# Second sample batch's logits in the last prompt step's slot, and two scale buffers in the second attention

## The reference

```python
fox_o = fox_prompt(fq, fk, fv, flf)                    # 8 heads x 64, causal, logits + forget bias
dsa_o = dsa_prompt(dq, iq, iw, dk, dv, ik, topk_prompt)  # 8 query heads on 2 kv heads, 256 picked keys
mix = jnp.concatenate([fox_o, dsa_o], axis=-1) @ w_out[l]
yp = post_sublayers(yp, mix, ...)                      # LN, FFN, LN
fox_s = fox_sample(gq, gk, gv, glf, cache_fox_k[l], cache_fox_v[l], cache_fox_logf[l])
dsa_s = dsa_select_attend(eq, jq, jw, pos_s, k_all, v_all, ik_all, kpos_s, topk_sample)
mix_s = jnp.concatenate([fox_s, dsa_s], axis=-1) @ w_out[l]
ys = post_sublayers(ys, mix_s, ...)
```

## Time and profile before

| what | us |
|---|---|
| three runs of before | 1408.16, 1414.36, 2643.92 (median 1414.36) |
| profiled execution, its own time | 1406.06 |
| its span, first to last instruction | 1404.2 |
| PE, PEld, DVE, ACT, POOL busy | 1343.7 (96%), 1199.1 (85%), 971.0 (69%), 686.7 (49%), 545.3 (39%) |
| mean granted PE clock | 0.991 of full speed |

### The profile page before, as it was taken

How to read it: one execution, slowest core, us unless ns; L and a number is a source line. 1 busy time by engine, 2 the same in 40 slices (tenths; PEclk the granted TensorE clock), 3 DMA queues, 4 the chain that set the end, 5 groups by cost and what they waited for, 6 DMA issues and landing times.

```text
span 1404.2 us, 23682 instructions
## 1 busy us (share of the span) xinstructions
PE 1343.7 (96%) x8916; PEld 1199.1 (85%) x8916; DVE 971.0 (69%) x1801; ACT 686.7 (49%) x1250; POOL 545.3 (39%) x518
## 2 busy tenths in 40 slices
PE   7989999989996999999989999999999999999997
PEld 7869999977775777787789999999999997678886
DVE  4489998878883889657866455555645557856498
ACT  5569989648773888611252232333223334524331
POOL 2407675512232022423465555555555551010011
PEclk9999999999998999999999999999999999999999
DMA  7202433349836312510134354355335459747454
GB/s 239 58 17 77 144 104 112 75 114 229 207 100 169 96 41 54 188 48 31 46 129 152 127 163 144 130 173 173 131 125 166 147 190 378 250 155 240 165 178 152
DMA packets 150354, 197.19 MB, mean 140 GB/s; under 512 B 28104, under 2 KB 106856, under 8 KB 150240
## 3 DMA queue, kind: packets, MB, share of 16 engines
q1 hardware_dynamic: 150240, 195.67, 44.6%
HBM read 136.69 MB, written 48.38 MB: 132 GB/s over the span
## 4 chain that ended last, share of the span: by engine, by line
PE 52%; DVE 3%; DMA 2%; issue 1%; ACT 1%; POOL 0%; POOLq 0%; SPq 0%; DVEq 0%; ACTq 0%
PE ffn L2760 31%; PE ffn L2269 6%; PE ffn L2860 4%; PE ffn L2862 4%; PE ffn L2861 4%; DMA down_raw<-in_w_down 1%; DVE rows L3256 1%; PE ffn L2734 1%; DVE down_lo L3125 0%; DMA up_raw<-in_w_up 0%; ACT down_hi L3016 0%; PE ffn L2879 0%; PE ffn L2877 0%; DVE h_T_lo L3160 0%; PE ffn L2285 0%
## 5 line engine op out<-in xcount | busy, mean ns | idle before, releaser
L3041 POOL TENSOR_TENSOR w_lo<-w_S,w_hi 128x512 fp32r<-128x512 f32 x88 | 119.2, 1355 | 108.9 <-ACT w_hi L2916 108.9
L2760 PE MATMUL ffn<-h_T_hi,w_hi 128*128 128x264 f32 x704 | 144.7, 285 | 0.2 <-DVE h_T_lo L3160 0.2
L3016 ACT CAST down_hi<-down_raw 128x1024 fp32r<-128x1024 f32 (+1 forms) x77 | 89.9, 1173 | 110.7 <-DMA down_raw<-down_w 46.2
L2760 PE MATMUL ffn<-h_T_lo,w_hi 128*128 128x264 f32 x704 | 143.7, 285 | 0.0
L2760 PE MATMUL ffn<-h_T_hi,w_lo 128*128 128x264 f32 x704 | 142.9, 283 | 0.0
L2916 ACT CAST w_hi<-w_S 128x512 fp32r<-128x512 f32 x88 | 54.8, 622 | 167.0 <-PE ffn L2760 147.4
L2173 POOL TENSOR_TENSOR ln_rstd<-ln_var_eps,ln_power 128x1 f32<-128x1 f32 (+1 forms) x18 | 29.4, 1633 | 272.9 <-DVE ln_var_eps L2153 141.0
L3125 DVE TENSOR_TENSOR down_lo<-down_raw,down_hi 128x1024 fp32r<-128x1024 f32 (+1 forms) x77 | 106.2, 1401 | 29.0 <-ACT down_hi L3016 28.3
L2860 PE MATMUL ffn<-down_hi 128*128 128x512 f32 x308 | 120.8, 392 | 3.7 <-DVE down_lo L3125 2.0
L2862 PE MATMUL ffn<-down_hi,down_lo 128*128 128x512 f32 x308 | 120.5, 391 | 0.0
L2861 PE MATMUL ffn<-down_lo,down_hi 128*128 128x512 f32 x308 | 120.4, 391 | 0.0
(11 more groups left out here) (423 smaller groups left out, 3841.5 us busy)
## 6 DMA issues: line engine op xcount, KB each, us to landing
down_raw<-down_a SPq DMA_DIRECT2D x77, 256.0 KB, 3.5
gate_raw<-in_w_gate SPq DMA_DIRECT2D x11, 1024.0 KB, 6.5
up_raw<-in_w_up SPq DMA_DIRECT2D x11, 1024.0 KB, 6.3
down_t<-in_w_down SPq DMA_DIRECT2D x44, 256.0 KB, 4.1
down_w<-down_t SPq DMA_DIRECT2D x22, 512.0 KB, 3.4
down_raw<-in_w_down SPq DMA_DIRECT2D x22, 512.0 KB, 6.2
down_raw<-down_w SPq DMA_DIRECT2D x44, 256.0 KB, 4.0
down_a<-down_s SPq DMA_DIRECT2D x10, 1024.0 KB, 4.1
```

What stands on the lines that cost most here:

```text
L2760: mm = nc.tensor.matmul(pp[:, bank[to] + ch, 0:PIECE], l, x[name][:, k, ch * PIECE:(ch + 1) * PIECE], start=opens and k == 0 and i == 0, s ...
L3016: nc.scalar.copy(hs[:, 0:n], raws[s % RAWS][:, 0:n]).then_inc(hi_done, 1)
L3041: nc.gpsimd.tensor_tensor(w_lo[n % 2][:, :, :], weight(m, SCHEME[q][0]), f32(w_hi[n % 2][:, :, :]), ALU.subtract).then_inc(w_lo_done, 1)
```

## The change

Three edits. First, in both attentions the logits of sample batch 17 move from slot L+3 to slot L, behind the last prompt step's transposes. Second, `attention` takes a list of scale buffers; the first attention gives it one, the second two, so that there SP waits for the multiplication two batches back. Third, to make room for the second buffer, `dsa_kT_new` and `dsa_q_diag` lie in another region of SBUF. The numbers of idle products stay as they are.

```diff
 def fox_ahead(batches):
     def ahead(batch):
         if batch.sample:
-            return [(1, 0, len(batch.parts) - 1)]
+            return [(1, 0, -1)]
...
-    [(1, 0, 2)]]
+    [(1, 0, -1)]]
...
+    scales_loaded = [sem(f"scales_loaded{i}") for i in range(len(scales))]
...
         def load_scales(batch):
             sp.wait_ge(scales_stored, 16 * (batch.b + 1))
-            if batch.b:
-                sp.wait_ge(normed, len(places(batch)) * batch.b)
-            sp.dma_start(scales[:, :], c["scale_rows"][batch.b].partition_broadcast(P)).then_inc(scales_loaded, 16)
+            s = batch.b % len(scales)
+            if batch.b >= len(scales):
+                sp.wait_ge(normed, len(places(batch)) * (batch.b - len(scales) + 1))
+            sp.dma_start(scales[s][:, :], c["scale_rows"][batch.b].partition_broadcast(P)).then_inc(scales_loaded[s], 16)
...
-            pool.wait_ge(scales_loaded, 16 * (batch.b + 1))
+            s = batch.b % len(scales)
+            pool.wait_ge(scales_loaded[s], 16 * (batch.b // len(scales) + 1))
...
-                nc.gpsimd.tensor_tensor(out, out, scale(scales), ALU.mult).then_inc(normed, 1)
+                nc.gpsimd.tensor_tensor(out, out, scale(scales[s]), ALU.mult).then_inc(normed, 1)
...
-        attention(nc, ctx, pl, [exp_a, exp_b, exp_c], scales, c, "fox", batches, filled(batches), fox_ahead(batches), source, loads, lambda pe: None,
+        attention(nc, ctx, pl, [exp_a, exp_b, exp_c], [scales], c, "fox", batches, filled(batches), fox_ahead(batches), source, loads, lambda pe: None,
...
-        scales = areas("dsa_scales", [P, 4 * P], F32)
-        kT_new = areas("dsa_kT_new", [P, 2, NEW], F32)
-        q_diag = areas("dsa_q_diag", [P, KV_H, P], F32)
+        scales = [areas(f"dsa_scales{s}", [P, 4 * P], F32) for s in range(2)]
...
+        q_diag = late("dsa_q_diag", [P, KV_H, P], F32)
+        kT_new = late("dsa_kT_new", [P, 2, NEW], F32)
```

More of the change, by code:

```diff
@@ L1349, in attention @@
     v_hi_done, v_lo_done = sem("v_hi_done"), sem("v_lo_done")
-    recip_done, scales_stored, scales_loaded = sem("recip_done"), sem("scales_stored"), sem("scales_loaded")
+    recip_done, scales_stored = sem("recip_done"), sem("scales_stored")
+    scales_loaded = [sem(f"scales_loaded{i}") for i in range(len(scales))]
     c["sems"] = {"freed": freed, "v_lo_done": v_lo_done, "qk_done": qk_done, "tr_done": tr_done, "pv_done": pv_done,
```

## The result

| | kernel before | changed kernel |
|---|---|---|
| median, us | 1410.53 (13 runs) | 1419.87 (13 runs) |
| lowest, us | 1407.62 | 1415.05 |
| profiled execution, span, us | 1404.2 | 1417.9 |

The ratio of the times is 1.0072, 95% interval 1.0057 to 1.0086. That is 10.2 us of 1410.5 (8.0 to 12.1): slower, beyond doubt, and within 2%. The prediction gave +6.4 us, a level of 1414 and a range of 1407 to 1421. The time lies in the range, near its upper end. One run of before took 2643.92 us, nearly twice the others, and so did one of the first experiment (2650.73); the comparisons leave both out.

What follows compares the result with a forecast made beforehand. PE was the busy engine, but other queues were taken to set the blocks' ends; 3.5 + 2.95 = +6.4 us on 1406.06 gave 1412.5, plus 2.1 made 1414.6, rounded to 1414; range 1407 to 1421.

Steps and rivals of the forecast that it cites:

- two scale buffers: Second attention: SP's waits for POOL go, but PE waits for nothing behind them and POOL stays covered; 0 us.
- the clock's fall: Rival, second attention: PE's clock drops to 1.2 GHz behind the new gap at slot L, +1.6 us, 1416; 22%.
- First seam: First attention's end: moved logits delay batch 14's joining, the scale load and the second attention's key rows; +3.5 us.
- step (d): First attention, ACT's program: batch 17's exponential ahead of batch 16's copy and batch 14's joining makes L1527 3.46 us late.
- Second seam: Second attention's end: PE waits for batch 16's maximum, then for batch 14's late joining, delaying the projection; +2.95 us.
- Placement: New places of `q_diag` and `kT_new`: same sizes and same instructions, 0 us.
- clock kept: Main case: both ends of the attentions late, PE's clock not falling behind the new gap; 1414 us, 55%.
- The level of the base: Whole kernel: forecast placed 2.1 us above the sum on the profiled execution, by the nearer of two undisturbed runs.
- Not slower: Rival, both attentions: PE loses its 0.31 and 0.66 us waits for exponentials, nothing else becomes late; 1407 us, 10%.
- Double buffering pays: Rival, second attention: earlier scale loads let POOL run ahead and PE get its slots sooner; 1413 us, 5%.
- Slower by over 2%: Rival, whole kernel: a 28 us loss, needing the clock at half rate for 56 us; 2%.
- The first three signs of the list: First attention's end in the profile: batch 17's maximum at about 427.1, L1527 of batch 14 at 430.3, scale load at 433.3.

Runs made afterwards that it cites:

- the first experiment: Kernel before, with only the first attention's logits of sample batch 17 moved to slot L, one scale buffer everywhere: ratio 1.0034 to the kernel before, +4.8 us.

## Why the prediction came out as it did

**The step that failed.** It is the placing of the forecast's level. The sum said +6.4 us, and the forecast was then placed by the nearer of two runs, at 1414, which is 0.4 us below the 1414.36 shown for the kernel before. As it stood it forecast no loss, and the runs showed one of 10.2 us (8.0 to 12.1). They also showed why: the median of before lies 4.5 us above its profiled execution, not 2.1. The sum itself was too small as well. Two of its terms were put at nothing: the two scale buffers at 0, which cost 0.66 us beside the moves, and the clock's fall, which was priced at 1.6 us as a rival and left out of the sum, and which costs 1.7 us in a part of the executions. The mechanism of the two seams was right in the main.

**Where the time went, point by point.**

- *First seam, forecast +3.5, measured 3.3 in the scale load, and 3.75 at the transposes in the first pair of traces (3.5 between the means).* Size and place are right: L1527 of batch 14 late, POOL late, SP's scale load late, rows late. That the chain is the cause is shown from two sides, by the second buffer in the first attention beside the moves and by the keys issued first. What step (d) left out is how the 3.3 us divide. It names ACT's order alone as the cause, since ACT is last; undoing that order takes back only 1.0 us, and 2.3 are PE's. Whoever had mended the change by step (d) would have been disappointed.
- *Second seam, the move alone, forecast +2.95, measured +3.0 in three traces* (20.95, 20.94 and 20.94 against 17.93 or 17.91). The path is right, with the gap 1.65 us where 2.06 was forecast, and the second gap 1.37 where it was about 1.6. That the number fits so well is partly luck: the joining was 2.8 us late and the last split 2.6, and 0.4 us came from POOL's multiplication beside that split, which the prediction had not seen.
- *Two scale buffers, forecast 0, measured +0.66 with the moves and +1.05 without them in the second seam.* This term was mis-sized. I asked who waits for POOL and found nobody, which is right. I did not ask what POOL runs beside once it is early. It runs beside DVE's splits, two of which then take 1.9 us instead of 1.2, and `finish` stands behind them. The Trainium skill's rule ("Trainium Kernel Development and Optimization", Best Practices, double buffering) fared worse than the 0: by itself the second buffer gained nothing that can be told from none, in the second attention (1.0001) or in the first (0.9985). Beside the moves, which make SP's wait in the first attention longer, it did take time out: the first seam was 23.60 us with it and 29.10 without.
- *Placement, forecast 0.* Right in the second seam: with the new places and one buffer in the second attention it takes 17.91 us without the moves and 20.94 with them, as with the old places.
- *The clock, priced at +1.6 us and given 22% as a rival.* It is not a rival that holds or does not hold, but something that comes in some executions and not in others: the changed kernel's own two traces show both. It happens in four of eight traces and costs 1.7 us, so as an estimate a median takes up roughly 0.9 us of it, or 1.4 us if the four of five with two buffers are the right share. That number belonged in the sum. My argument against it, one gap of 2.1 us as the only witness, gave no ground for "clock kept" either.
- *The level of the base, the step that failed.* I put the forecast 2.1 us above the profiled execution because the nearer of two runs lay there. Thirteen runs centre 4.5 us above it (1410.53 against 1406.06). With the same +6.4 that gives 1416.9 instead of 1414. Two runs 6.2 us apart can't place a median to 2 us, and choosing the nearer brought the forecast down to the level of the 1414.36 shown for before, as if nothing were lost.

**The sum as the runs give it.** 3.3 (first seam) + 3.0 (second move) + 0.7 (buffers, with the moves) + 0.9 (half of the clock's fall) = 7.9 us (8.4 with 1.4 for the clock), against 7.8 (4.9 to 10.6) in the one comparison and 10.2 (8.0 to 12.1) in the other. The sum lies at the lower edge of the second interval, 7.9 just below it and 8.4 just within. No trace shows a third place: the stretch between the seams differs by 0.76 us, the rest by -0.67, and both lie within what the other traces show there (123.5 to 125.6, and 811.8 to 816.0). Whether the larger figure holds more than scatter stays open.

**The other rivals.** *Not slower* fell: none of the kernels with a moved logit and the old links is below +3 us. It asked for batch 17's exponential 3.5 us earlier than slot L allows, and slot L gave its start at M + 4.2 us, as reckoned. *Double buffering pays* fell with the buffers alone at 1.0001. *Slower by over 2%* had nothing behind it.

**What was asked of the profile.** The first three signs of the list came true, counted from M to take the scatter out: maximum 2.93 us after it (forecast 427.1 - 424.14 = 3.0), copy 5.99 (6.2), scale load 9.04 (9.2). SP's waits for POOL in the second attention are down to one of 4.7 us. POOL ends ahead of DVE, by nearly five microseconds. The projection's first product, forecast at 596.0, stands at 603.93; without the 6.19 us ahead of the change and the 0.76 between the seams that is 596.98, 1.0 us beyond the forecast, of which the buffers are 0.66.

## What to carry to other kernels

When an instruction's lateness is to be explained, work out the arrival of every engine that feeds it, from rows; two that come within a microsecond hide one another, and removing one gives only the difference. Ask of a buffer that frees an idle engine not only who waits for it, but what it will run beside. And a block that ends in idleness before a transfer is asking for its place in the queue to be changed: moving eight issues ahead of one wait gave more (6 to 8 us) than anything that was done to the engines' order.

## What the hardware showed beyond expectation

- DVE's splits of 128x1024 fp32 and POOL's multiplications of 64x256 hold each other up one at a time. A split takes 1.23 us if it starts first and up to 1.9 us if it starts beside a running multiplication; a multiplication takes 0.85 us with no split beside it and up to 1.9 us if one has just begun. The mean of the three splits, 1.6 us, is a mixture of the two.
- TensorE's clock is not a function of the program alone. With the same instructions ahead and gaps of 1.65 and 1.76 us it stayed at 1.00 in one execution and fell to 0.51 in the other; over all traces it fell behind gaps of 1.71, 1.72, 1.76 and 2.09 us and stayed behind 1.65, 1.69 and 1.74.
- SP's issues of the key rows mostly take 0.4 to 0.6 us each, but the fourth of the eight takes 2.24 to 5.05 us in every one of the eleven traces that issue them behind the 24 queries. What holds it is not shown. It hides small gains from issuing earlier: 2.1 us earlier at the scale load brought nothing at the transposes.
- Unchanged code in front of the change took from 423.4 to 432.9 us in thirteen traces. A difference of two single spans says nothing about a term of a few microseconds; a difference counted from a landmark just ahead of the change does.
